# A hybrid layer: two latents turned by VectorE and a trip through DRAM instead of by TensorE, angles and sines moved up

## The reference, cut to what matters

```python
h = rms_norm(x, attn_norm_w)
hq, hf, hi, hg, c_q, c_kv, k_r = jnp.split(h @ w_in, IN_SPLITS, axis=-1)   # c_q, c_kv: 512 columns each
q  = (rms_norm(c_q, q_norm_w) @ w_uq).reshape(B_, S_, MLA_HEADS, QK_DIM)
kv = (rms_norm(c_kv, kv_norm_w) @ w_ukv).reshape(B_, S_, MLA_HEADS, QK_NOPE + V_DIM)
ang = positions[..., None] * inv_freq                                     # cos, sin: for q and k
...
x = x + concat([o_a, o_b]) @ w_out
x = x + (silu(gate) * up) @ w_down
```

## Time and profile before

| | us |
|---|---|
| median of 3 runs (lowest, highest) | 1108.22 (1107.96, 1108.38) |
| the profiled execution | 1107.74 |
| its span, first to last instruction | 1106.0 |
| TensorE busy in the span | 1096.4 (99%) |
| VectorE, ScalarE, GpSimd busy | 903.1, 645.8, 65.2 |

### The profile page before, as it was taken

The page is one execution under the profiler, slowest core; times in us unless marked ns, Lnnn a source line. Parts: engine busy times, 40 slices in busy tenths (PEclk is TensorE's granted clock), DMA queues, the critical chain, the costliest instruction groups (busy, mean ns, idle before and its releaser), DMA issues.

```text
span 1106.0 us, 15243 instructions
## 1 busy us (share of the span) xinstructions
PE 1096.4 (99%) x5126; PEld 922.6 (83%) x5126; DVE 903.1 (82%) x1249; ACT 645.8 (58%) x907; POOL 65.2 (6%) x164
## 2 busy tenths in 40 slices
PE   8999999999999999999999999999999999999998
PEld 8988888888888878888888888888888888888887
DVE  6688787587876587688888988988988889999887
ACT  6676776668654466365455455554554555654553
POOL 1500000000000010001101101001011010000000
PEclk9999999999999999999999999999999999999999
DMA  8966455554645486766777777777777777666665
GB/s 305 289 186 206 129 169 166 151 160 155 229 171 187 155 239 194 229 220 210 248 231 223 240 232 222 230 234 217 235 236 226 239 264 236 218 214 206 197 202 171
DMA packets 108083, 234.21 MB, mean 212 GB/s; under 512 B 8448, under 2 KB 17408, under 8 KB 107776
## 3 DMA queue, kind: packets, MB, share of 16 engines
q1 hardware_dynamic: 101360, 211.34, 59.2%
q0 software_dynamic: 6528, 22.03, 6.9%
q10 hardware_dynamic: 144, 0.20, 0.1%
HBM read 221.99 MB, written 11.53 MB: 211 GB/s over the span
## 4 chain that ended last, share of the span: by engine, by line
PE 97%; DVE 1%; ACT 0%; issue 0%; DMA 0%; DVEq 0%; ACTq 0%
PE side L2029 24%; PE main L1798 22%; PE side L2031 12%; PE main L1801 11%; PE side L1999 4%; PE side L2000 4%; PE side L2001 4%; PE main L2001 3%; PE main L2000 3%; PE main L1999 3%; PE main L1818 2%; PE side L1924 1%; PE side L1840 0%; PE side L1875 0%; PE side L1876 0%
## 5 line engine op out<-in xcount | busy, mean ns | idle before, releaser
L1048 ACT CAST w_hi<-raw 128x1024 fp32r<-128x1024 f32 x245 | 240.2, 986 | 157.2 <-PE side L2029 80.3
L1637 DVE TENSOR_TENSOR w_lo<-raw,w_hi 128x1024 fp32r<-128x1024 f32 x245 | 274.6, 1133 | 15.1 <-ACT w_hi L1048 15.0
L1159 DVE TENSOR_TENSOR w_lo<-raw,w_hi 128x1024 fp32r<-128x1024 f32 (+3 forms) x156 | 178.8, 1155 | 93.4 <-ACT w_hi L826 91.8
L826 ACT CAST w_hi<-raw 128x1024 fp32r<-128x1024 f32 (+3 forms) x155 | 153.5, 999 | 125.1 <-PE main L1798 111.3
L1798 PE MATMUL main<-w_hi,hT_hi 128*128 128x512 f32 (+2 forms) x416 | 160.9, 388 | 0.0
L1801 PE MATMUL main<-w_hi,hT_lo 128*128 128x512 f32 (+2 forms) x416 | 157.6, 380 | 0.0
L2029 PE MATMUL side<-w_hi,hT_hi 128*128 128x512 f32 x400 | 155.6, 389 | 0.0
L2031 PE MATMUL side<-w_hi,hT_lo 128*128 128x512 f32 x400 | 155.6, 389 | 0.0
L1798 PE MATMUL main<-w_lo,hT_hi 128*128 128x512 f32 (+2 forms) x416 | 107.1, 379 | 0.0
L2029 PE MATMUL side<-w_lo,hT_hi 128*128 128x512 f32 x400 | 106.9, 389 | 0.0
L1801 PEld LDWEIGHTS main<-w_hi,hT_lo 128*128 128x128 f32 x416 | 78.2, 188 | 13.0
(11 more groups left out here) (305 smaller groups left out, 1882.8 us busy)
## 6 DMA issues: line engine op xcount, KB each, us to landing
raw<-in_w_gate_up SPq DMA_DIRECT2D x176, 512.0 KB, 4.9
raw<-in_w_down SPq DMA_DIRECT2D x88, 512.0 KB, 4.4
raw<-in_w_in SPq DMA_DIRECT2D x64, 512.0 KB, 4.3
raw<-in_w_out SPq DMA_DIRECT2D x32, 512.0 KB, 3.7
raw<-in_w_in SPq DMA_DIRECT2D x15, 384.0 KB, 5.5
squares<-hiddenT POOLq DMA_DIRECT2D x11, 512.0 KB, 4.7
hiddenT<-squares POOLq DMA_DIRECT2D x44, 128.0 KB, 5.5
raw<-in_w_ukv SPq DMA_DIRECT2D x8, 512.0 KB, 4.4
```

What stands on the lines that cost most here:

```text
L826: copy(w_hi[:, slot, 0:n], raw[:, slot, 0:n]).then_inc(s_hi, 1)
L1048: copy(w_hi[:, n % RING, 0:cols], src).then_inc(s_hi, 1)
L1159: tt(w_lo[:, slot, 0:n], raw[:, slot, 0:n], w_hi[:, slot, 0:n].bitcast(F32), ALU.subtract)\
L1637: tt(w_lo[:, n % RING, 0:cols], src, w_hi[:, n % RING, 0:cols].bitcast(F32), ALU.subtract)\
```

## The change

The two steps `lat_t` of each latent go. VectorE turns the 32x32 blocks of the scaled latent in one instruction right behind `lat_b` (`lat_turn`, at 23 and 27), into the storage of `hkT` or `hgate`, which are not in use yet. SP sends the result to a scratch tensor in DRAM behind the loads of granules 31 and 36, and brings it back in four transfers behind those of 33 and 38, after a wait for the way out. ScalarE and VectorE split what came back in the new step `lat_back`, at 30 and 34. The angles move from 29 to 14 and the sines from 30 to 15; the positions are loaded behind granule 12, the other two small loads move up by one granule, and the waits of `angles` for all constants and all small loads move to `kr_b`. TensorE waits for the identity once, ahead of its first granule.

```diff
@@ -208,7 +208,10 @@
 
 XT_AFTER = {1: (1,), 2: (2,), 3: (3, 4), 4: (5,), 5: (6,), 6: (7,), 7: (8,)}
 X_AFTER = {11: 0, 13: 1, 15: 2, 17: 3}
+POS_AFTER = 12
 SMALL_AFTER = 20
+LAT_OUT_AFTER = (31, 36)
+LAT_BACK_AFTER = (33, 38)
 
 X_SPLIT = (FIRST, FIRST + 1, -1, 0, 1, 2, 3, 4, 5)
 
@@ -230,9 +233,10 @@
     for i in range(2):
         e = END[("lat", i + 1)]
         e += 0 if i else 4
-        s += [(e + 1, ("lat_a", i)), (e + 2, ("lat_b", i))] + [(e + 5, ("lat_t", i, n)) for n in range(2)]
+        s += [(e + 1, ("lat_a", i)), (e + 2, ("lat_b", i)), (e + 2, ("lat_turn", i))]
+        s += [((30, 34)[i], ("lat_back", i, n)) for n in range(2)]
     e = END[("lat", 2)]
-    s += [(e + 1, ("kr_a",)), (e + 4, ("angles",)), (e + 5, ("sines",)), (e + 9, ("kr_b",))]
+    s += [(e + 1, ("kr_a",)), (14, ("angles",)), (15, ("sines",)), (e + 9, ("kr_b",))]
 
     s += [(e + 7, ("lb_a", 0)), (e + 13, ("lb_b", 0)), (e + 15, ("lb_c", 0))]
     e = END[("ukv", 2)]
...
@@ -450,6 +454,8 @@
         chunk_decay = mb("chunk_decay", [P, NT, GW // CHUNK])
         hS = mb("hS", [P, GH, 3, P])
         latents = (lat, hv)
+        latents_in_blocks = [v[:, :, :].rearrange("p t c -> p (t c)").rearrange("p (a x) -> p a x", a=P // Q)
+                             for v in (hkT, hgate)]
         qTn = X[:, 0, :].rearrange("p (h t) -> p h t", h=HEADS)
         kTn = X[:, 1, :].rearrange("p (h t) -> p h t", h=HEADS)
         mix.close()
...
@@ -618,11 +629,11 @@
             return v.rearrange("p t c -> p (t c)")
 
 
-        small_loads = [(pos_i[:, :], positions[0].rearrange("(t p) -> p t", p=P)),
-                       (qw_row[:, :], q_head_norm_w[0].partition_broadcast(P)),
+        small_loads = [(qw_row[:, :], q_head_norm_w[0].partition_broadcast(P)),
                        (kw_row[:, :], k_head_norm_w[0].partition_broadcast(P))]
         N_SMALL = len(small_loads)
         N_IDENT = 2
+        N_FREQ = 2 + 3 + HALF
         N_CONST = 2 + 3 + 1 + 2 * 3 * LEVELS + 2 + 2 + HALF
 
 
@@ -646,9 +657,26 @@
                     cols = slice(NB * X_AFTER[g], NB * (X_AFTER[g] + 1))
                     sp.dma_start(X[:, :, cols], x_v[:, :, cols]).then_inc(s_x[X_AFTER[g]], 16)
 
+                if g == POS_AFTER:
+                    sp.dma_start(pos_i[:, :], positions[0].rearrange("(t p) -> p t", p=P),
+                                 allow_slow_non_contiguous=True).then_inc(s_pos, 16)
+
                 if 0 <= g - SMALL_AFTER < N_SMALL:
                     dst, src = small_loads[g - SMALL_AFTER]
                     sp.dma_start(dst, src, allow_slow_non_contiguous=True).then_inc(s_small, 16)
+
+                if g in LAT_OUT_AFTER:
+                    i = LAT_OUT_AFTER.index(g)
+                    sp.wait_ge(s_latturned, i + 1)
+                    sp.dma_start(lat_scratch[i].rearrange("a c b x -> (a c) b x"), latents_in_blocks[i])\
+                        .then_inc(s_latout[i], 16)
+
+                if g in LAT_BACK_AFTER:
+                    i = LAT_BACK_AFTER.index(g)
+                    sp.wait_ge(s_latout[i], 16)
+                    for b in range(P // Q):
+                        sp.dma_start(latents_in_blocks[i][Q * b:Q * (b + 1), :, :],
+                                     lat_scratch[i][:, :, b, :].rearrange("a c x -> c a x")).then_inc(s_latback[i], 16)
 
             for j in range(GU):
                 half, k = divmod(j, KT // 2)
@@ -900,10 +928,12 @@
                         square(latents[i][:, t, :], sumsq[:, t:t + 1], scale=r_in[:, t:t + 1])
                 elif kind == "lat_b":
                     root(("lat_a",) + a, NT)
-                elif kind == "lat_t":
+                elif kind == "lat_back":
                     i, j = a
-                    ps, k, col = filled(s), 4 * i + 2 * j, (V_KVN if i else V_QN) + 2 * j
-                    split_hi([(mT_hi[:, k + n, :], ps[:, n * SEQ:(n + 1) * SEQ], col + n) for n in range(2)])
+                    act.wait_ge(s_latback[i], MOVED)
+                    src = latents_in_blocks[i].rearrange("p a (t k r) -> p k t a r", t=NT, r=Q)
+                    split_hi([(mT_hi[:, 4 * i + k, :].rearrange("p (t a r) -> p t a r", t=NT, r=Q), src[:, k, :, :, :],
+                               (V_KVN if i else V_QN) + k) for k in (2 * j, 2 * j + 1)])
                 elif kind == "kr_a":
                     for t in range(NT):
                         square(krw[:, t, :], sumsq_kr[:, t:t + 1])
@@ -955,7 +985,7 @@
                     dst, fn = {"hq": (hq, ACT.Silu), "hf_a": (hlf, ACT.Sigmoid), "hi": (hv, ACT.Copy),
                                "hg": (hgate, ACT.Silu)}[kind]
                     if kind == "hq" and not a[0]:
-                        act.wait_ge(s_side, USE[("lat_t", 0, 1)] + 1)
+                        act.wait_ge(s_latturned, 1)
                     if a[0] and kind == "hg":
                         act.wait_ge(s_given["dve"], GIVEN[USE[("o_a", 0, NT - 1)]])
                     for t in range(NT):
@@ -1216,8 +1246,8 @@
 
             def angles():
 
-                dve.wait_ge(s_small, 16 * N_SMALL)
-                dve.wait_ge(s_const, N_CONST)
+                dve.wait_ge(s_pos, 16)
+                dve.wait_ge(s_const, N_FREQ)
                 link(nc.vector.tensor_copy(pos_f[:, :], pos_i[:, :]))
                 for t in range(NT):
                     for f in range(2):
@@ -1285,13 +1315,29 @@
                     for t in range(NT):
                         v = latents[a[0]][:, t, :]
                         ts(v, v, inv[:, t:t + 1], None, ALU.mult).then_inc(s_lat, 1)
-                elif kind == "lat_t":
+                elif kind == "lat_turn":
+                    i = a[0]
+                    dve.wait_ge(s_lat, NT * (i + 1))
+                    nc.vector.transpose(latents_in_blocks[i].rearrange("p b (n r) -> p n b r", r=Q),
+                                        latents[i][:, :, :].rearrange("p t (k b c) -> p (t k) b c", b=P // Q, c=Q))\
+                        .then_inc(s_latturned, 1)
+                elif kind == "lat_back":
                     i, j = a
-                    ps, k, col = filled(s), 4 * i + 2 * j, (V_KVN if i else V_QN) + 2 * j
-                    split_lo(s, [(mT_lo[:, k + n, :], ps[:, n * SEQ:(n + 1) * SEQ], mT_hi[:, k + n, :], col + n)
-                                 for n in range(2)])
+                    dve.wait_ge(s_latback[i], MOVED)
+                    dve.wait_ge(s_thi, SPLIT[s] + 1)
+                    src = latents_in_blocks[i].rearrange("p a (t k r) -> p k t a r", t=NT, r=Q)
+                    for k in (2 * j, 2 * j + 1):
+                        col = (V_KVN if i else V_QN) + k
+                        for t in range(NT):
+                            hi, lo = [v[:, 4 * i + k, t * P:(t + 1) * P].rearrange("p (a r) -> p a r", r=Q)
+                                      for v in (mT_hi, mT_lo)]
+                            ins = stt(out=lo, in0=src[:, k, t, :, :], scalar=vec_cols[:, col:col + 1],
+                                      in1=hi.bitcast(F32), op0=ALU.mult, op1=ALU.subtract)
+                    ins.then_inc(s_tlo, 1)
                 elif kind == "kr_b":
                     b = BLOCK_OF[("lat", 2)]
+                    dve.wait_ge(s_small, 16 * N_SMALL)
+                    dve.wait_ge(s_const, N_CONST)
                     dve.wait_ge(s_taken[b % 2], taken(b))
                     link(tt(krw[:, :, :], krw[:, :, :],
                             kw_row[:, NOPE:QK].unsqueeze(1).to_broadcast([P, NT, ROPE]), ALU.mult))
@@ -1847,11 +1893,6 @@
                     b = BLOCK_OF[("out2", c)]
                     pe.wait_ge(s_taken[b % 2], taken(b))
                     turn_x(s, 4 * c + 2 * j)
-                elif kind == "lat_t":
-                    i, j = a
-                    pe.wait_ge(s_const, N_IDENT)
-                    pe.wait_ge(s_lat, NT * (i + 1))
-                    turn_x(s, 2 * j, latents[i])
                 elif kind in ("q_t", "k_t"):
                     j, b = a[0], int(kind == "k_t")
                     pe.wait_ge(s_stage, 2 * j + b + 1)
@@ -1967,6 +2008,7 @@
                     return hT_hi, hT_lo, [12 + k for k in ks]
                 return (mT_hi, mT_lo, ks) if kind == "uq" else (hT_hi, hT_lo, ks)
 
+            pe.wait_ge(s_const, N_IDENT)
             for g, (b, k, n) in enumerate(GRANULES):
                 for s in steps_at(g):
                     step(s)
```

More of the change, by code:

```diff
@@ L302, in side_uses @@
     kind = step[0]
-    if kind in ("x2", "lat_t", "o_t"):
+    if kind in ("x2", "o_t"):
         return [(step, "dve")]
@@ L327 @@
             GIVEN[USE[_key]] = _given[_engine]
-SPLITS = [step for _, step in SCHEDULE if step[0] in ("x", "x2", "x_back", "lat_t", "o_t", "attend")]
+SPLITS = [step for _, step in SCHEDULE if step[0] in ("x", "x2", "x_back", "lat_back", "o_t", "attend")]
 SPLIT = {step: n for n, step in enumerate(SPLITS)}
@@ L352, in split_needed @@
     if kind == "uq":
-        return SPLIT[("lat_t", 0, 1)] + 1
+        return SPLIT[("lat_back", 0, 1)] + 1
```

(7 more changed lines are left out.)

## The result

The kernel after takes 1112.76 us in the median (1112.22 to 1115.89, 5 runs), the kernel before beside it 1108.10 (1107.74 to 1108.38, 5 runs): ratio 1.0046, interval 1.0034 to 1.0057. It is 4.7 us slower, where 1108.5 was forecast and the range ended at 1112.0. Its profiled execution took 1112.54 us, with a span of 1110.8 and a granted clock of 1.0.

What follows compares the result with a forecast made beforehand. TensorE's matmuls were taken to bound the kernel (97% of the span). Transposes -1.8, angles +0.6, what is late next +0.5 and trip +1.2 sum to +0.5 us, giving 1108.5 us, range 1106.1 to 1112.0.

Steps and rivals of the forecast that it cites:

- The transposes: TensorE's eight transposes per latent, on the path: removing them saves 0.92 us each, 1.8 us for both.
- The angles' term: Angles and sines moved up: TensorE loses 0.6 us at granules 19 to 21, between nothing and 1.2.
- The way from angle to sine to cast 19: ScalarE's sines wait for the angles, so cast 19 moves from 38.52 to 42.40 and TensorE loses 0.1 us.
- granule 18 is in time: Behind the moved angles, VectorE's lo 18 ends by 41.5, where TensorE wants it at 42.10.
- What is late next: Front end's lead gone and VectorE's turn before lo 27: 0.5 us lost at granule 27, between nothing and 1.3.
- The trip's term: Latents' trip through DRAM: 1.2 us lost before granule 38 by the second latent, between nothing and 3.9.
- Granule 33 lost nothing: First latent's split is ready by 74.8, 77.4 at the latest, and granule 33 starts at 77.3: no loss.
- The price that the prediction estimated from the Trainium skill: Transfer of 128 KB in 2.3 us; with it the trip's term would be nothing and the sum 1107.0.
- A: Rival, the forecast: short waits at granules 19 to 21, 27 and 38 repay the gain; 1107 to 1110.3, chance 0.52.
- C: Rival: slower by ScalarE's wait for the second latent before cast 38; 1110.4 to 1112, chance 0.16.
- B: Rival: gain stands, transfers home in 3.2 to 4.5 us and front end regains its lead; 1105.9 to 1107, chance 0.22.
- D: Rival: slower by weight loads landing after 9.7 us instead of 4.1 among the trips; 1110.5 to 1114, chance 0.07.

Runs made afterwards that it cites:

- e6: Kernel after with all GpSimd constants made before its wait for X and the sines at granule 25: 0.9 us over before, ratio 1.0005.
- e10: e7 measured again, to narrow its interval: 1.2 us below before, ratio 0.9991.
- e12: e6 with the rotation of kr moved from granule 34 to 41: 0.5 us over before, ratio 1.0007.
- e11: The kernel after, unchanged, measured again beside the kernel before: 1113.01 us against 1108.29, ratio 1.0040.
- e5: Kernel after with all GpSimd constants (masks and the two large zero fills) made before its wait for X: 1111.86 us, ratio 1.0030.
- e2: Kernel before with only angles and sines moved to granules 14 and 15 and positions loaded behind granule 12: 1111.84 us, ratio 1.0024.
- e7: e6 with the second latent's split moved from granule 34 to 40: 0.9 us below before, ratio 0.9992.
- e3: Kernel after with GpSimd's masks made before its wait for X, the two large zero fills left behind it: 1114.61 us, ratio 1.0049.

## Why the prediction was wrong

The time fell outside the range because every term that was to be lost was too small in the sum. The rows of the kernel after give -1.8 for the transposes, +2.1 for the angles (0.6 forecast), +1.6 for what is late next (0.5 forecast) and +2.2 for the trip (1.2 forecast): +4.0 instead of +0.5.

**The transposes: right.** 0.92 us each were forecast from the starts; e6 to e10 and e12 show 1.83 for both, 114 ns a turn. The Trainium skill's 390 ns for a bf16 tile (VectorE: DVE Perf Modes, The three transpose paths), by which 6.2 us would have come free by the prediction's estimate, doesn't hold for these float32 turns amid other matmuls.

**The angles' term: mis-sized, the larger failure.** I took 0.6 us for granules 19 to 21, and 1.2 at the most, "if the angles take some 10% longer beside GpSimd's making of masks". They took 32% longer (6.2 for 4.69), and the term measured 2.1 (1.8 in e11). The way from angle to sine to cast 19 was right: with GpSimd out of the way (e5) the term measures 0.5. The bound failed because the 10% had no source: in the trace of before the angles ran with GpSimd idle, so it had no row of the effect. The step's claim that granule 18 is in time failed with it (0.74 us waited).

**What is late next: right place, not the whole.** 0.5 was forecast at granule 27, within 0 and 1.3. Granules 27 and 28 lost 1.0 in the first profile and less than 0.1 in e11's. The same lost lead took 0.6 at granule 35, by ScalarE's drain behind a late cast 36, which I had not followed.

**The trip's term: right place, wrong end of the chain.** I took 1.2 us at granule 38 by the second latent's landing. Granule 38 lost 0.4, granule 39 1.8: 2.2. I followed VectorE's queue to rest 38 and stopped; the next thing behind it that TensorE wants is the first query's `stage_r`, and it had less slack than granule 38. The kernel before showed that, in the last step of `stage_r`, and in TensorE's start of granule 38 and its transposes of that query:

```profile
92.36 0.28 DVE L1215 TENSOR_TENSOR stage_r<-rot 128x128 f32<-128x128 f32 x1
```

```profile
90.42 0.39 PE L1798 MATMUL main<-w_hi,hT_hi 128*128 128x512 f32 x1
...
93.15 0.60 PE L1862 MATMUL side<-ident,stage 128*128 128x128 f32 x4
```

`stage_r` was ready at 92.64, 0.5 us ahead of the transposes; rest 38 was ready at 88.09, 2.3 us ahead of granule 38 (90.42). The landing, on which I spent the term, cost 0.5 of the 2.2 us; the split's 1.7 us on ScalarE and 2.1 on VectorE, which I counted against granule 38 only, cost the other 1.7. Granule 33 lost nothing in the kernel after, as forecast. The price that the prediction estimated from the Trainium skill (DMA: Bandwidth & Descriptors, Anatomy of one DMA) is given there for transfers that GpSimd issues, as X's trips are; the latents' went by SP. Their shortest landing, 2.7 us, came near its 2.3, and no row of mine was that short.

**The rivals.** A's mechanism, short waits that pay the gain back, is what happened, but the waits came to 5.8 us (4.0 + 1.8) against a gain of 1.8, not to 2.3. C put the slower side down to ScalarE's wait for the second latent: its place was right, but that wait is 0.5 of the 2.2 us. B had the transfers right (3.1 us in the middle for the second way back) and the time wrong: the gain went. D's loads of 9 us did not come, but its mechanism was there in small: the weight loads issued from 57 to 90 us landed after 4.7 to 5.7 us in the middle in the twelve profiles with the trip, and after 3.9 and 3.7 in the two without it (before, e2). In e7 this cost TensorE nothing.

## What to carry to other kernels

Before a step is moved to another time, list what the other engines do at that time: two fills on GpSimd (1.40 and 0.97 us) held a VectorE conversion of 0.16 us for 3.05, and its time in the old place said nothing of the new one. That holds for the step that makes room, too: the constants that I moved out of the way met VectorE's first weight cast. Follow a new piece of work through the queue past the next wait to everything that TensorE will ask of that queue, and do so on both engines that it lengthens. The version that keeps the gain in TensorE's rows differs from this change by three places in an order (constants made early, sines where ScalarE idles, the second split behind the first query), not by its idea; constants made between the first cast and the angles are untested.

## What the runs showed of the hardware

A VectorE conversion of 128x2 elements took 0.16 us (e5), 0.65 (after) and 3.05 (e3) by what GpSimd did meanwhile, and a weight cast of 128x384 took 0.36 or 0.70 to 0.84; scalar operations of 128x128 went from 0.23 to 0.47 and 0.55, and those with two tensors and a scalar hardly changed (1.93 to 1.97 for six). One issue of SP, among four of the first way back, took 1.49 us where others took 0.43. Weight loads of 384 and 512 KB issued from 57 to 90 us landed 0.8 to 2.0 us later in the middle in the twelve profiles with the latents' trips (4.7 to 5.7) than in the kernel before (3.9). Starts of loops in the feed-forward part showed neighbouring matmuls up to 0.53 us apart instead of 0.23 in the kernel after and up to 1.1 in e3, where the profile names a wait of 0.7 us for a weight's rest (L1683), and nothing of the kind in e6 and e11.
